# Second feed-forward block begun with a seven-product quad, with raw weight parts first in every quad

## Time and profile before

| | before |
|---|---|
| median of 3 runs | 986.85 us (986.82 to 986.89) |
| the profiled execution's own time | 986.68 us |
| its span | 985.0 us |
| TensorE busy | 976.0 us |
| VectorE busy | 756.1 us |
| ScalarE busy | 481.0 us |
| GpSimd busy | 204.0 us |

### The profile page before, as it was taken

The page is one execution under the profiler, slowest core; times in us unless marked ns, Lnnn a source line. Parts: engine busy times, 40 slices in busy tenths (PEclk is TensorE's granted clock), DMA queues, the critical chain, the costliest instruction groups (busy, mean ns, idle before and its releaser), DMA issues.

```text
span 985.0 us, 15298 instructions
## 1 busy us (share of the span) xinstructions
PE 976.0 (99%) x6074; PEld 863.2 (88%) x6074; DVE 756.1 (77%) x921; ACT 481.0 (49%) x670; POOL 204.0 (21%) x172
## 2 busy tenths in 40 slices
PE   9999999999999999999999999999999999999997
PEld 7799889998999878878788878889988999889986
DVE  5888578985698788765579796798966899568964
ACT  6655225552355556664455753545532565325543
POOL 1003002220032222222064361201210223002321
PEclk9999999999999999999999999999999999999999
DMA  9516314562133343434443132263452335513312
GB/s 267 148 58 163 106 32 112 141 154 87 37 109 92 86 129 87 129 92 125 145 130 108 52 99 86 76 160 86 127 154 63 87 94 156 136 43 87 113 38 87
DMA packets 192270, 105.42 MB, mean 107 GB/s; under 512 B 4052, under 2 KB 189496, under 8 KB 192200
## 3 DMA queue, kind: packets, MB, share of 16 engines
q1 hardware_dynamic: 191528, 103.40, 37.7%
q10 hardware_dynamic: 672, 1.05, 0.3%
HBM read 102.30 MB, written 2.13 MB: 106 GB/s over the span
## 4 chain that ended last, share of the span: by engine, by line
PE 97%; DVE 1%; ACT 1%; issue 1%; DVEq 0%; POOL 0%; POOLq 0%
PE bank L1681 12%; PE bank L1683 12%; PE bank L1682 12%; PE bank L1616 9%; PE bank L1618 9%; PE bank L1617 9%; PE bank L1700 8%; PE bank L1701 8%; PE bank L1699 8%; PE bank L1842 1%; PE bank L1771 1%; PE bank L1849 1%; PE bank L1765 1%; PE bank L1768 1%; PE bank L1829 0%
## 5 line engine op out<-in xcount | busy, mean ns | idle before, releaser
L611 POOL TENSOR_TENSOR post<-post,rstd 128x256 f32<-128x256 f32 x57 | 93.1, 1632 | 516.3 <-DVE post L1142 516.3
L1681 PE MATMUL bank<-thi,w_hi_part 128*128 128x256 f32 x608 | 167.8, 276 | 0.0
L1682 PE MATMUL bank<-tlo,w_hi_part 128*128 128x256 f32 x608 | 167.8, 276 | 0.0
L1683 PE MATMUL bank<-thi,w_lo_part 128*128 128x256 f32 x608 | 167.8, 276 | 0.0
L1052 DVE TENSOR_TENSOR w_lo_part<-w_raw,w_hi_part 128x1024 fp32r<-128x1024 f32 (+1 forms) x102 | 129.8, 1274 | 18.3 <-ACT w_hi_part L699 16.1
L1699 PE MATMUL bank<-acthi,w_hi_part 128*128 128x512 f32 x340 | 132.7, 390 | 0.0
L1701 PE MATMUL bank<-acthi,w_lo_part 128*128 128x512 f32 x340 | 132.3, 389 | 0.0
L1700 PE MATMUL bank<-actlo,w_hi_part 128*128 128x512 f32 x340 | 132.3, 389 | 0.0
L1681 PE MATMUL bank<-xfhi,w_hi_part 128*128 128x256 f32 x418 | 115.6, 277 | 0.0
L1682 PE MATMUL bank<-xflo,w_hi_part 128*128 128x256 f32 x418 | 115.5, 276 | 0.0
L1683 PE MATMUL bank<-xfhi,w_lo_part 128*128 128x256 f32 x418 | 115.4, 276 | 0.0
(11 more groups left out here) (293 smaller groups left out, 2081.9 us busy)
## 6 DMA issues: line engine op xcount, KB each, us to landing
w_raw<-in_ffn_w_gate SPq DMA_DIRECT2D x42, 512.0 KB, 4.0
w_raw<-in_ffn_w_up SPq DMA_DIRECT2D x42, 512.0 KB, 5.1
w_raw<-in_ffn_w_down SPq DMA_DIRECT2D x32, 512.0 KB, 5.1
w_raw<-in_w_in SPq DMA_DIRECT2D x29, 512.0 KB, 3.8
w_raw<-in_w_out SPq DMA_DIRECT2D x16, 512.0 KB, 4.0
w_raw<-in_ffn_w_down SPq DMA_DIRECT2D x16, 384.0 KB, 4.3
decay<-acs_rows SPq DMA_DIRECT2D x16, 256.0 KB, 4.6
out<-xtok SPq DMA_DIRECT2D x4, 512.0 KB, 2.6
```

Of the source, the lines that this page charges most:

```text
L1681: pe.matmul(out, w, hi, start=opens and e == 0 and k == 0, stop=False, skip_group_check=True)
L1682: pe.matmul(out, w, lo, start=False, stop=False, skip_group_check=True)
L1683: mm = pe.matmul(out, wl, hi, start=False, stop=end, skip_group_check=True)
```

## The change

DIRECT_TILES of the second block becomes 0: it has 11 quads and no direct tile. The parts of every quad, in both blocks, now run as A11, A12, SUM1, SUM2, SUM3, SUM4, A22; the copies on ScalarE and the follow-up work on VectorE are attached to the parts of the new order. The eight output units ahead of the second block are computed in the order 0, 4, 1, 5, 2, 6, 3, 7, with the token combinations and the first sums of weights among them. The statistic of the norm is taken after SUM1 of the first quad, the root and the reciprocal follow some parts later. The semaphores that product waits for, and which bank each part uses, stay as they were.

```diff
-DIRECT_TILES = (4, 2)
+DIRECT_TILES = (4, 0)
-A11, SUM1, SUM2, A12, SUM3, SUM4, A22 = range(PARTS)
+A11, A12, SUM1, SUM2, SUM3, SUM4, A22 = range(PARTS)
+OUT_ORDER = (0, 4, 1, 5, 2, 6, 3, 7)
...
 ScalarE, ffn:
-                    if it.kind == "product" and it.part == SUM1:
+                    if it.kind == "product" and it.part == A12:
                         copy_product(q, A11, 0, q % 2, p1_read, act0_ready)
                     if it.kind == "product" and it.part == SUM2:
                         copy_product(q, SUM1, 1, 2, p5_read, act22_ready)
-                    if it.kind == "product" and it.part == A12:
+                    if it.kind == "product" and it.part == SUM3:
                         copy_product(q, SUM2, 2, q % 2, u2_read, act0_ready)
...
-                    if f and it.kind == "direct" and it.raw == 0:
-                        combination_hi(1, KH - 1)
+                    if f and r == 3:
+                        rms(2)
...
 ScalarE, output units:
+            for i, d in enumerate(OUT_ORDER):
+                if i % 2 == 0:
+                    halves_of_x(1, d, R_N2)
+                norm_hi(2, d, R_N2, seen=i)
+                if i == DK - 1:
+                    combination_hi(1, KH - 1)
+                square(2, i, i % 2, xT[:, cols(d)])
+                convert(M + U_OUTS + i + RING)
+                if i % 2 and i < DK - 1:
+                    combination_hi(1, i // 2)
...
 VectorE, ffn:
-                    if f and it.kind == "direct" and it.raw:
-                        combine_low(1, it.raw)
+                    if f and r == 4:
+                        inverse(2)
+                    if chained and it.part == A12:
+                        act_even(q - 1)
                     if chained and it.part == SUM1:
-                        act_even(q - 1)
+                        act_low(f, QUADS[q - 1].tile, 0)
                     if chained and it.part == SUM2:
-                        act_low(f, QUADS[q - 1].tile, 0)
                         act21(q - 1)
-                    if chained and it.part == A12:
                         act22(q - 1)
...
 VectorE, output units:
+            first = DIRECT_QUADS
+            for i, d in enumerate(OUT_ORDER):
+                dve.wait_ge(unit_done, i + (M + U_OUTS + 1))
+                dve.tensor_tensor(xT[:, cols(d)], PB[4 + i % 2][:, :], xT[:, cols(d)], ALU.add).then_inc(x_ready, 1)
...
+                if i == DK - 2:
+                    first_sum(first)
+                if i == DK - 1:
+                    norm_lo(2, d, R_N2, seen=i)
+                if i % 2:
+                    dve.wait_ge(x_ready, i + (2 * DK + 1))
+                    combine(1, i // 2, R_N2)
+                elif i:
+                    combine_low(1, i // 2 - 1)
+                if i < DK - 1:
+                    norm_lo(2, d, R_N2, seen=i)
+                    convert(M + U_OUTS + i + RING)
+            second_sum(first)
+            combine_low(1, KH - 1)
+            convert(M_FFN2 + SUM2)
+            third_sum(first)
...
 TensorE, product:
+                if n == M_FFN2:
+                    pe.wait_ge(xg_lo, 3 * DK - 1)
+                if f and local == 0 and part == A12:
+                    pe.wait_ge(xg_lo, 3 * DK)
+                order = [(e, k) for e in range(2) for k in range(KH)]
+                if f and local == 0 and part == SUM1:
+                    order = [(e, k) for k in range(KH) for e in range(2)]
...
 TensorE, ffn:
-                        if n == M_FFN2:
-                            stat(2)
                     if it.kind == "product":
                         product(f, it, n)
+                        if n == M_FFN2 + SUM1:
+                            stat(2)
```

More of the change, by code:

```diff
@@ L557, in _ @@
                 mix_fetch(U_OUTP + i, w_out[:, DK:2 * DK, block(i)])
-            for i in range(DK):
-                mix_fetch(U_OUTS + i, w_out[:, 0:DK, block(i)])
+            for i, d in enumerate(OUT_ORDER):
+                mix_fetch(U_OUTS + i, w_out[:, 0:DK, block(d)])
             ffn_fetch(1)
@@ L712, in convert, with norm_hi @@
                     act.activation(whi[:, slot(n), 0:blocks], raw[:, it.raw % RAW, 0:blocks], ACT.Copy).then_inc(w_hi, 1)
-            def norm_hi(p, d, gain):
-                act.wait_ge(x_ready, d + (DK * p + 1))
+            def norm_hi(p, d, gain, seen=None):
+                act.wait_ge(x_ready, (d if seen is None else seen) + (DK * p + 1))
                 act.activation(normed(p)[0][d], xT[:, cols(d)], ACT.Copy,
@@ L801, in ffn @@
                         silu_even(q - 1)
-                    if chained and it.part == SUM2:
+                    if chained and it.part == SUM1:
                         split_act(q - 1, 0)
@@ L1053, in convert, with norm_lo @@
                                       whi[:, slot(n), 0:blocks].bitcast(F32), ALU.subtract).then_inc(w_lo, 1)
-            def norm_lo(p, d, gain):
-                dve.wait_ge(xg_hi, d + (DK * p + 1))
+            def norm_lo(p, d, gain, seen=None):
+                dve.wait_ge(xg_hi, (d if seen is None else seen) + (DK * p + 1))
                 dve.scalar_tensor_tensor(out=normed(p)[1][d], in0=xT[:, cols(d)], scalar=par[:, one(d + gain)],
@@ L1537, in _ @@
                         dve.reciprocal(cbuf[:, g, :], cbuf[:, g, :]).then_inc(grstd_ready, 1)
[L1538 to L1541, removed]
-                    dve.wait_ge(neg_ready, 2)
[L1543 to L1549, removed]
+            first = DIRECT_QUADS
+            for i, d in enumerate(OUT_ORDER):
+                dve.wait_ge(unit_done, i + (M + U_OUTS + 1))
+                dve.tensor_tensor(xT[:, cols(d)], PB[4 + i % 2][:, :], xT[:, cols(d)], ALU.add).then_inc(x_ready, 1)
+                if i == 1:
+                    dve.wait_ge(neg_ready, 2)
+                if i == DK - 2:
[14 more added lines that the diff above has]
+            third_sum(first)
             def tokens(d, e):
@@ L1630, in direct @@
                     pe.wait_ge((g_scaled, act_ready)[it.part], tile - 1)
-                products(PB[bank][:, :], n, 0, UB, *normed(2 * f), ready=(xg_lo, 2 * DK) if n == M_FFN2 else None)
+                products(PB[bank][:, :], n, 0, UB, *normed(2 * f))
             def moving(f, part, k):
@@ L1672, in product @@
                 pe.wait_ge(w_lo, n + 1)
-                for e in range(2):
-                    out = bank[:, half(e)]
[L1675 to L1683, removed]
+                if n == M_FFN2:
[5 more added lines that the diff above has]
+                    order = [(e, k) for k in range(KH) for e in range(2)]
+                for i, (e, k) in enumerate(order):
+                    out = bank[:, half(e)]
+                    if part == SUM1 and local == 0 and e == 0:
+                        pe.wait_ge(t_lo, KH * f + k + 1)
+                    hi, lo = moving(f, part, k)
+                    w, wl = whi[:, slot(n), e * KH + k, :], wlo[:, slot(n), e * KH + k, :]
+                    end = k == KH - 1
+                    pe.matmul(out, w, hi, start=opens and i == 0, stop=False, skip_group_check=True)
+                    pe.matmul(out, w, lo, start=False, stop=False, skip_group_check=True)
+                    mm = pe.matmul(out, wl, hi, start=False, stop=end, skip_group_check=True)
                 mm.then_inc(unit_done, 1)
```

3 lines of the change are left out of this document (1 added, 2 removed).

## The result

The changed kernel takes 1006.94 us, the median of 4 runs (1005.53 to 1007.33); the kernel before took 986.84 us beside it (986.34 to 986.89). The ratio is 1.0203, with a 95% interval of 1.0191 to 1.0216: slower, by 20.1 us. The interval lies clear of 1 and on both sides of 1.02. The forecast was 1004.0, in a range of 1000.5 to 1010. The profiled execution took 1006.96 us, 20.28 us more than that of before.

A forecast was written before the change was run, and what follows sets the result against it. TensorE was taken to bound the kernel, so every wait put there lengthens it. Bubbles of 17.9 us and -0.7 at the second block's start gave +17.2 on 986.68, shown as 1004.0 us; range 1000.5 to 1010.

The forecast's parts named there:

- part 2: New order of parts in all quads: uncovered copy between SUM2 and SUM3 costs 0.94 us, 17.9 us in 19 quads.
- The weight load: At SUM3's wait: a load pulled ahead would give a 0.84 us bubble, 2 us less over 19; 0.10 was kept.
- part 3: Second block's first quad: ends at 660.2 against 660.89 for the direct units, -0.7 us with its bubbles.
- its ends of -2.3 and +2.6: Second block's first quad: -2.3 us if its bubble is short, +2.6 if the whole reciprocal fell into TensorE's path.
- The queue: Second block's first quad: ScalarE's conversions, SUM1's copy and the root delay SUM2's copy to 651.9, a 2.5 us bubble.
- its sign of being right: In the profile after: clock at the upper level, beside 20 copy waits, 20.0 us quads and 60 copies.
- part 1: Second block's two direct tiles become a quad: saves 3.28 us by work alone, extra conversions, sums, copies and gathers free.
- the saving of 3.28 us: Second block: direct units' 23.22 us less 0.86 for the statistic and 19.08 for a quad.
- the rival that kept the whole saving: Between SUM2 and SUM3: copy hidden after all, no wait, quad's saving stays, 983.5 us; chance 0.02.
- The rival of the clock: Behind the pauses in 20 quads: granted clock falls for one unit each, 55 us more, 1059; chance 0.03.
- The rival of a late copy: At SUM2's end in every quad: ScalarE isn't free, 0.5 us more each makes 10 us, 1014; chance 0.10.

The follow-up runs named there:

- the kernel with the covered copy and the halves: The changed kernel with SUM1 moved behind SUM2 to cover its copy, and the first quad's reciprocal made in two halves: 987.49 us, ratio 1.0011.

## Why the prediction was right, and where it was off

The direction, the mechanism and its place held; the time was 2.9 us above the forecast of 1004.0 and inside the range.

**The bubble (part 2).** Predicted 0.94 us, measured 0.96 at the matmuls around it and 0.98 from quad to quad. Its terms: the copy's start 0.03 to 0.04 after the drain, the copy 0.60, take-up 0.05 (assumed 0.04), restart 0.10 (taken 0.10). The prediction's "next matmul at 1.05 instead of 0.11" puts the restart one matmul too early: the first comes at 0.97 and the second at 1.19 behind the last start of SUM2, and the sum is the same. The wait itself is 0.69 us, not "some 0.9", because the drain ahead of it isn't idle time. 19 quads made 18.6 us, 17.9 predicted: +0.7 of the miss. The 60 copies and the 19.08 + 0.98 = 20.06 us between quads are those written down; ScalarE was idle for 1.17 us ahead of the copy, where 1.2 had been worked out.

**The weight load.** The sentence of the Trainium skill on loads pulled ahead ("TensorE: Matmul & The Clock Gate", "Architectural detail: the array is 16× 32×32, not 1× 128×128") would have given a bubble of 0.84, had it held past this wait. Here the load at 683.12 starts with its matmul, behind the wait, and the waits of weight loads for the copy add up to 19.5 us in 20 cases. At this kind of wait nothing was pulled past it.

**The start of the second block (part 3).** This is the step that failed in size: -0.7 predicted, +1.66 measured, 2.4 us off and within its ends of -2.3 and +2.6. The queue itself was right, instruction by instruction. From SUM2's last matmul to SUM3's first it was 2.82 us where the prediction has 2.5 + 0.11 = 2.61. The copy ended at 661.39 - 8.80 = 652.59 on the prediction's time axis, not 651.9, for one reason in VectorE's timeline:

```profile
653.48 1.99 DVE L1051 TENSOR_TENSOR w_lo_part<-wsum,w_hi_part 128x1024 fp32r<-128x1024 f32 x1 [0.24 <-ACT w_hi_part L711]
```

The low part of SUM2's weights took 1.99 us, not 1.22, beside an addition of GpSimd (652.66, 1.73 us), and everything behind moved by 0.7. SUM2 itself ended later too, at 649.9 on that axis instead of 649.5, so the pause is only 0.2 longer. The other 0.4 us is the slower pace of matmuls told of below and two steps of 0.19 at 649.13. The large piece is the clock, 1.60 us, which the prediction had put at nothing in this pause: its sign of being right was a clock at the upper level, and the page's 40 slices still show that, while the stretches of 1 us do not. The quad ended 24.88 us after its start, not 22 to 23. Together 0.2 + 0.1 (the restart) + 0.4 + 1.6 = 2.3 of the 2.4.

**The work that was said to cost nothing (part 1).** "They cost nothing as long as VectorE and ScalarE keep up, which they do in quads already" does not hold for this group. Once the copy is covered, the saving of 3.28 us does not appear: the group takes 80.79 us, not 77.2. "In quads already" was read from the later quads (18.2 of 19.08 us); the block's first two keep VectorE longer, 41.0 us for TensorE's 39.0 in the kernel with the covered copy. In the changed kernel the three later quads of the group take 20.06 us each, the bare copy's price and no more, so the pauses seem to have hidden the shortage, and the forecast did not suffer by it. That was luck as far as this term goes; the rival that kept the whole saving (983.5) was wrong about that too, beside the copy.

**The rival of the clock.** It was the wrong size, but not wrong altogether. After 19 pauses of 0.69 us the clock stayed at the upper level, as it did after 1.31 when the copy was made twice; after the one of 2.54 us it fell. The Trainium skill ("TensorE: Matmul & The Clock Gate", "A second HAM failure mode: psum-queue depth-cycling") describes, for another kernel, oscillation from short idle times between groups of matmuls that cycle through banks. These traces do not bear that out at 0.69 us every 20 us.

**The rival of a late copy** had its place only in the first quad, where the prediction had put it, and nowhere else: the longest of the 19 others is 0.7 us.

## What to carry to other kernels

When parts accumulate on one bank and an engine must read it in between, put one independent part of another bank behind the read: 2.7 us of cover make a copy of 0.6 us free, and no cover costs 0.98, drain, two hand-ons and restart included. Before a busy engine's work is called free in a new place, add up the group's work on every engine against the time that is wanted: here VectorE was busy for 77 us beside TensorE's 77.2, for 41.0 beside 39.0 in the first two quads, and a saving of 3.3 us never appeared. Which of VectorE's load and the late rstd was the cause isn't shown. A pause at a block's start is priced with the granted clock behind it, and one that is removed may come back one quad later.

## What had not been expected of the hardware

**The clock after one pause.** After 2.54 us without a matmul the granted clock fell to 0.50 for about 3.5 us, from 0.4 us behind the pause on; after 3.4 us (the copy made twice) it did so again, from 1.4 us behind it on. After pauses of 0.69, 1.0, 1.2, 1.31, 1.7 and 2.19 us in these kernels it stayed at 1.00. Here is the stretch behind the pause of 2.19 (the new start with the old order) and then one behind that of 3.4:

```profile
644.93:648.00 3.07, 3.07 (x26) 3.07 (x27) 2.89 (x2) 2.09 (x4) 1.09 (x1) 1.00 0.35 86
```

```profile
669.00:671.00 2.00, 2.00 (x13) 2.00 (x12) 2.00 (x1) 0.00 (x0) 0.00 (x0) 0.57 1.18 307
```

**Two paces at the full clock.** Matmuls of 256 columns start 0.113 us apart in most stretches and 0.118 in some, with the granted clock at 1.00 in both. In the changed kernel the slower pace holds from 649.5 to 658.6 us, outside the waits; with the new start and the old order from 649 to 682, where it costs 1.2 us; with the copy ahead of its queue from 671 to 681. It often begins where TensorE has just taken up work after a break, and it ends without a change in the instructions. Its cause is open, and no run was made for it.
